# Decay rows spread over the partitions by DMA instead of by TensorE, with one exponential on 32 rows

## The reference

```python
# state space, per head, within a chunk of 128; a = dt * a_head
a_cum = jnp.cumsum(a, axis=-1)
seg = a_cum[..., :, None] - a_cum[..., None, :]
Lmat = jnp.exp(jnp.where(causal, seg, -jnp.inf))
CB = jnp.einsum('bclgn,bcsgn->bgcls', Cc, Bc)
y_diag = jnp.einsum('bgcls,bgecls,bcsgep->bclgep', CB, Lmat, X)
y_off = jnp.einsum('bclgn,bcgepn,bgecl->bclgep', Cc, prev, jnp.exp(a_cum))
# delta rule, per head, within a chunk of 64
G = jnp.cumsum(gc, axis=-1)
gamma = jnp.exp(jnp.where(tri, G[..., :, None] - G[..., None, :], -jnp.inf))
A = jnp.where(strict, jnp.einsum("bnhid,bnhjd->bnhij", kc * bc[..., None], kc) * gamma, 0.0)
```

## Time and profile before

| | |
|---|---|
| median of 3 runs | 2864.24 us (2861.77 to 2864.45) |
| the profiled execution, its own time | 2860.19 us |
| its span in the profile | 2858.4 us |
| TensorE busy | 2618.0 us, 92% |
| VectorE busy | 1500.9 us, 53% |
| ScalarE busy | 1125.3 us, 39% |
| GpSimd busy | 125.9 us, 4% |
| moved by DMA | 209.93 MB, 73 GB/s over the span |

### The profile page before, as it was taken

The page is one execution under the profiler, slowest core; times in us unless marked ns, Lnnn a source line. Parts: engine busy times, 40 slices in busy tenths (PEclk is TensorE's granted clock), DMA queues, the critical chain, the costliest instruction groups (busy, mean ns, idle before and its releaser), DMA issues. The chain is left out here.

```text
span 2858.4 us, 33690 instructions
## 1 busy us (share of the span) xinstructions
PE 2618.0 (92%) x13778; PEld 2044.9 (72%) x13778; DVE 1500.9 (53%) x2280; ACT 1125.3 (39%) x1687; POOL 125.9 (4%) x98
## 2 busy tenths in 40 slices
PE   8999978998998999988999978988898997899998
PEld 6888846766776776767888846756667675688886
DVE  5444266656566664345443254587644445466632
ACT  4222234555544455443222234242424255344422
POOL 0000020000000000010000020000000000100000
PEclk9999989999999999999999988999999998999999
DMA  4333312221221221222233311111111110233332
GB/s 139 97 102 91 101 52 69 67 68 58 82 72 47 74 67 59 82 81 74 96 96 98 94 54 59 53 52 38 52 38 45 60 59 23 74 96 96 98 99 76
DMA packets 59193, 209.93 MB, mean 73 GB/s; under 512 B 6560, under 2 KB 6560, under 8 KB 59040
## 3 DMA queue, kind: packets, MB, share of 16 engines
q1 hardware_dynamic: 57600, 204.38, 22.8%
q10 hardware_dynamic: 1440, 3.41, 0.3%
HBM read 205.66 MB, written 2.10 MB: 73 GB/s over the span
## 5 line engine op out<-in xcount | busy, mean ns | idle before, releaser
L1349 PE MATMUL bank<-uR,hl 128*128 128x512 f32 x2232 | 923.2, 414 | 54.5 <-DVE uR L1962 27.1
L1350 PE MATMUL bank<-uR,hl 128*128 128x512 f32 x2232 | 885.6, 397 | 0.0
L1351 PE MATMUL bank<-uR,hl 128*128 128x512 f32 x2232 | 884.5, 396 | 0.0
L1950 DVE TENSOR_TENSOR hl<-raw,hl 128x1024 fp32r<-128x1024 f32 (+1 forms) x391 | 473.1, 1210 | 618.1 <-ACT hl L1668 617.3
L1349 PEld LDWEIGHTS bank<-uR,hl 128*128 128x128 f32 x2232 | 429.0, 192 | 189.9 <-issue 67.5
L1668 ACT CAST hl<-raw 128x1024 fp32r<-128x1024 f32 (+1 forms) x391 | 402.4, 1029 | 249.4 <-PE bank L1351 248.3
L1351 PEld LDWEIGHTS bank<-uR,hl 128*128 128x128 f32 x2232 | 428.2, 192 | 93.7
L1350 PEld LDWEIGHTS bank<-uR,hl 128*128 128x128 f32 x2232 | 429.2, 192 | 85.9 <-issue 5.2
L1349 PE MATMUL bank<-act,hl 128*128 128x512 f32 x528 | 205.4, 389 | 0.0
L1350 PE MATMUL bank<-act,hl 128*128 128x512 f32 x528 | 205.4, 389 | 0.0
L1351 PE MATMUL bank<-act,hl 128*128 128x512 f32 x528 | 205.4, 389 | 0.0
(11 more groups left out here) (434 smaller groups left out, 2595.3 us busy)
## 6 DMA issues: line engine op xcount, KB each, us to landing
raw<-in_win SPq DMA_DIRECT2D x147, 512.0 KB, 3.5
raw<-in_w SPq DMA_DIRECT2D x44, 512.0 KB, 3.5
raw<-in_w1g SPq DMA_DIRECT2D x22, 512.0 KB, 3.5
raw<-in_w1u SPq DMA_DIRECT2D x22, 512.0 KB, 3.5
raw<-in_w2g SPq DMA_DIRECT2D x22, 512.0 KB, 3.5
raw<-in_w2u SPq DMA_DIRECT2D x22, 512.0 KB, 3.5
raw<-in_w1d SPq DMA_DIRECT2D x16, 512.0 KB, 3.5
raw<-in_wssd SPq DMA_DIRECT2D x16, 512.0 KB, 3.6
```

Source lines behind the costliest of these rows:

```text
L1349: e.matmul(s.bank[:, :], h[:, 0, w], hi, start=s.first and q == 0, stop=False)
L1350: e.matmul(s.bank[:, :], h[:, 0, w], lo, start=False, stop=False)
L1351: i = e.matmul(s.bank[:, :], h[:, 1, w], hi, start=False, stop=s.last and q == n - 1)
L1950: e.tensor_tensor(h[:, 1, 0:s.width], x[:, 0:s.width], h[:, 0, 0:s.width].bitcast(F), ALU.subtract).then_inc(*sig("dve_split.lo", s))
```

## The change

The rows are spread by DMA. A new step `spread`, issued by ScalarE, copies rows of a page in SBUF to a page over 128 or 2 x 64 partitions; it waits for the row, for the readers of the slot's last use (8 semaphore slots, taken in turn) and for the page's last readers. In the state space the copies of a round (two E of one row each, one EA of two rows) are issued together: round 0 ahead of `ssd_x`, round 1 ahead of the four rounds, rounds 2 and 3 after `ssd_y` of rounds 0 and 1. EA's exponential is no longer taken on 128 partitions each time: `decay` takes it once on the 32 rows into a page `eac`, whose rows are copied. In the delta rule both spreads of a pair are issued at the start of `gdn_prep`. VectorE's subtraction and minimum of a head become four instructions of 128 columns that do both. The pages `ac` and `eac` are held to the end of the fourth group, the pools have 27 in place of 24 extra pages, and `mR` pages 16 and 17, `idR`, `selR`, `ssd_sel` and the step that filled `idR` go.

```diff
-NB1, NB2, NA = 24, 24, 11
+NB1, NB2, NA = 27, 27, 11
+NROW = 8
...
+    def spread(to, src, ready, rows):
+        n = row_next["n"] % NROW
+        row_next["n"] += 1
+        use = row_uses[n]
+        step("spread", to=to, src=src, ready=ready, rows=rows, slot=n, free=list(use[1]))
+        use[0] += 16 * len(rows)
+        to.t = [(f"row{n}_in", None, use[0])]
+        return n
...
     def ssd_core(g):
...
+        def begin(e2):
+            for hh in (2 * e2, 2 * e2 + 1):
+                E = fp.take()
+                Es.append((E, spread(E, ac, ac.t, [(8 * g + hh, 0, 128)])))
+            EA = fp.take()
+            EAs.append((EA, spread(EA, eac, eac.t, [(8 * g + 2 * e2, 0, 64), (8 * g + 2 * e2 + 1, 64, 64)])))
+
+        begin(0)
...
+        begin(1)
         for e2 in range(4):
-            b, EA, b2 = SB.take(), fp.take(), SB.take()
+            b2, (EA, n) = SB.take(), EAs[e2]
...
-            yield
+            if e2 < 2:
+                begin(e2 + 2)
+            yield
...
     def gdn_prep(p, hs):
+        gm, AT = fp.take(), gp.take()
+        n = spread(gm, nar, nar.t, [(2 * p, 0, 64), (2 * p + 1, 64, 64)])
+        n2 = spread(AT, nar, nar.t, [(32 + 2 * p, 0, 64), (33 + 2 * p, 64, 64)])
         yield from both(l2(k[0], 1.0, k2, 0), l2(k[1], 1.0, k2, 1), l2(q[0], DSC), l2(q[1], DSC))
...
 TensorE
-        def ssd_front(s):
-            one = idR[0:32, s.H:s.H + 1].broadcast_to([32, 128])
-            e.matmul(s.b[:, :], one, mR[0][0:32, 16, :], start=True, stop=False)
-            e.matmul(s.b[:, :], one, mR[0][0:32, 17, :], start=False, stop=True).then_inc(*sig("pe_ssd.cum", s))
...
-            e.matmul(s.b[:, :], selR[:, s.i, :], mR[0][0:32, 16, :], start=True, stop=False)
-            e.matmul(s.b[:, :], selR[:, s.i, :], mR[0][0:32, 17, :], start=False, stop=True).then_inc(*sig("pe_ssd.ea", s))
...
-                t = e.matmul(s.b[r, :], con[1][0:32, h:h + 1].broadcast_to([32, 64]), s.nar[0:32, :], start=True, stop=True)
...
-                t = e.matmul(s.bb[r, :], con[1][32:64, h:h + 1].broadcast_to([32, 64]), s.nar[32:64, :], start=True, stop=True)
...
 ScalarE
-            e.copy(mR[0][0:32, 16, :], s.ac[0:32, :]).then_inc(*sig("act_ssd.achi", s))
+            after(*s.eac.after)
+            activate(s.eac[0:32, :], s.ac[0:32, :], ACT.Exp).then_inc(*sig("act_ssd.eac", s))
+
+        def spread(s):
+            after(*s.ready, *s.free, *s.to.after)
+            for row, first, n in s.rows:
+                e.dma_start(s.to[first:first + n, :], s.src[row:row + 1, :][:, None, :].broadcast_to([1, n, L])).then_inc(sem(f"row{s.slot}_in"), 16)
...
-            activate(s.EA[:, :], s.b[:, :], ACT.Exp).then_inc(*sig("act_ssd.EA", s))
...
 VectorE
-            e.tensor_tensor(v3(s.E), v3(s.b), over(n3(acN)[:, :, s.H][:, :, None], 128), ALU.subtract).then_inc(*sig("dve_ssd.seg", s))
-            e.tensor_scalar(s.E[:, :], s.E[:, :], 0.0, None, ALU.min).then_inc(*sig("dve_ssd.min", s))
+            after(*s.et)
+            for t in range(T4):
+                x = e.tensor_scalar(s.E[:, tcol(t)], s.E[:, tcol(t)], n3(acN)[:, t, s.H:s.H + 1], 0.0, ALU.subtract, ALU.min)
+            x.then_inc(*sig("dve_ssd.min", s))
...
-            e.tensor_tensor(v8(s.gm), v8(s.b), col(gcol, s.p), ALU.subtract).then_inc(*sig("dve_gdn.seg", s))
+            e.tensor_tensor(v8(s.gm), v8(s.gm), col(gcol, s.p), ALU.subtract).then_inc(*sig("dve_gdn.seg", s))
...
-            e.tensor_tensor(s.AT[:, :], s.gm[:, :], s.bb[:, :], ALU.mult).then_inc(*sig("dve_gdn.beta", s))
+            e.tensor_tensor(s.AT[:, :], s.AT[:, :], s.gm[:, :], ALU.mult).then_inc(*sig("dve_gdn.beta", s))
```

More of the change, by code:

```diff
@@ L324, in rstd @@
         return r
+    row_uses = [[0, []] for _ in range(NROW)]
+    row_next = {"n": 0}
+    def spread(to, src, ready, rows):
[6 more added lines that the diff above has]
+        return n
     def side_rstd(src, which):
@@ L569, in decay_side @@
         dt = S1["dt"]
-        e1, w, ln, a, ac = fp.take(), fp.take(), fp.take(), fp.take(), fp.take()
-        s = step("decay", dt=dt, e1=e1, w=w, ln=ln, a=a, ac=ac, after=t_phase)
+        e1, w, ln, a, ac, eac = fp.take(), fp.take(), fp.take(), fp.take(), fp.take(), fp.take()
+        s = step("decay", dt=dt, e1=e1, w=w, ln=ln, a=a, ac=ac, eac=eac)
+        ac.t, eac.t = [("dve_ssd.scan", s)], [("act_ssd.eac", s)]
         e1.release(("dve_soft.s5", s))
@@ L581, in decay_side @@
         dt.release(("pe_ssd.decay", s2))
-        ac.release(("pe_ssd.decay", s2), ("dve_ssd.aclo", s))
-        S1["decay"], S1["cum"] = s2, s
+        S1["decay"], S1["ac"], S1["eac"] = s2, ac, eac
     def project_group(g):
@@ L598, in project_group @@
         yield
-    S1["sel"] = []
     def ssd_core(g):
@@ L604, in ssd_core @@
         xs, B, C = G["xs"], G["B"], G["C"]
-        dec, cum = S1["decay"], S1["cum"]
-        s_sel = step("ssd_sel", g=g, after=list(S1["sel"]))
-        Xd = []
+        dec, ac, eac = S1["decay"], S1["ac"], S1["eac"]
+        Xd, Es, EAs = [], [], []
+        def begin(e2):
[5 more added lines that the diff above has]
+        begin(0)
         for t in range(T4):
@@ L630, in front @@
         def front(hh):
-            b, E = SB.take(), fp.take()
-            s = step("ssd_front", H=8 * g + hh, b=b, E=E, CB=CB, cum=cum, dec=dec)
+            E, n = Es[hh]
+            s = step("ssd_front", H=8 * g + hh, E=E, et=list(E.t), CB=CB, dec=dec)
             E.t = [("dve_ssd.E", s)]
-            b.release(("dve_ssd.seg", s))
-            return E
-        Es = [front(0)]
+            row_uses[n][1] = list(E.t)
+        front(0)
         yield
-        Es.append(front(1))
+        front(1)
         yield
@@ L666, in ssd_core @@
             EA.release(*Y[e2].t)
-            S1["sel"] = [("pe_ssd.ea", s_f)]
+            row_uses[n][1] = list(Y[e2].t)
             yield
             if e2 < 3:
-                Es += [front(2 * e2 + 2), front(2 * e2 + 3)]
+                front(2 * e2 + 2)
+                front(2 * e2 + 3)
                 yield
             yb = SB.take()
-            s_y = step("ssd_y", e2=e2, Xd=Xd, E=[Es.pop(0), Es.pop(0)], yb=yb, Y=Y[e2], yt=list(Y[e2].t))
+            s_y = step("ssd_y", e2=e2, Xd=Xd, E=[Es[2 * e2][0], Es[2 * e2 + 1][0]], yb=yb, Y=Y[e2], yt=list(Y[e2].t))
             for x in s_y.E:
@@ L988, in gdn_prep @@
             yield
-        gb, gm = SB.take(), fp.take()
-        s1 = step("gdn_decay", p=p, nar=nar, cols=cols, b=gb, gm=gm)
-        gb.release(("dve_gdn.seg", s1))
+        s1 = step("gdn_decay", p=p, cols=cols, gm=gm, gt=list(gm.t))
+        row_uses[n][1] = [("dve_gdn.seg", s1)]
         yield
-        bb, AT, kk, qk = SB.take(), gp.take(), SB.take(), SB.take()
-        s2 = step("gdn_att", p=p, nar=nar, k=k2, q=q, bb=bb, AT=AT, kk=kk, qk=qk, gm=gm, s=s1)
-        bb.release(("dve_gdn.beta", s2))
+        kk, qk = SB.take(), SB.take()
+        s2 = step("gdn_att", p=p, k=k2, q=q, AT=AT, at=list(AT.t), kk=kk, qk=qk, gm=gm, s=s1)
+        row_uses[n2][1] = [("dve_gdn.beta", s2)]
         AT.t = [("dve_gdn.AT", s2)]
@@ L1916, in scalar_program @@
               "conv": conv, "decay": decay, "decay_turn": decay_turn, "ssd_cb": ssd_cb, "ssd_state": ssd_state,
-              "ssd_front": ssd_front, "ssd_from": ssd_from, "silu_ev": silu_ev, "tanh_ev": tanh_ev, "half_ev": half_ev,
+              "ssd_front": ssd_front, "spread": spread, "silu_ev": silu_ev, "tanh_ev": tanh_ev, "half_ev": half_ev,
               "qkv_ev": qkv_ev, "gate_out": out_hi, "att_out": out_hi, "merge1": out_hi, "merge2": out_hi, "lam": lam_,
@@ L2146, in ssd_from @@
         def ssd_from(s):
-            go.wait_ge(*on("act_ssd.EA", s))
+            after(*s.et)
             go.wait_ge(*on("pe_ssd.off", s))
```

58 lines of the change are left out of this document (11 added, 47 removed).

## The result

| | before | after |
|---|---|---|
| median | 2864.34 us (2861.77 to 2864.68) | 3086.99 us (3085.10 to 3087.44) |
| ratio, 95% interval | | 1.0778 (1.0759 to 1.0797) |
| span of the profiled execution | 2858.4 us | 3085.2 us |
| TensorE busy | 2618.0 us | 2621.7 us |

The change costs 222.6 us. Lines moved: L1349, L1350, L1351 of before are now L1376, L1377, L1378; `ssd_x` is L1416, the matmuls of `ssd_from` L1441, `ssd_y` L1450; ScalarE's split is L1671 and VectorE's L1948; the copies are issued at L1769. VectorE's multiplication with `CB`, the last step to `E`, is L2138, and every activation of ScalarE is L1654. The median before is of four runs here, one more than ahead of the prediction.

The account below looks back on a forecast made before the run. TensorE's instruction order bounds the kernel; with copies, four state-space groups need 477.6 us instead of 347.2, +130.4, less the delta rule's 8.5: +122, 2986 us. The 8-in-10 range was 2820 to 3085.

Parts of the forecast that it names:

- what is removed: TensorE: matmuls taken out save 32.8 us in four state-space groups and 8.5 in the delta rule, 41.3 us of work.
- VectorE nothing: State-space heads: four 128-column instructions add 1 to 17 us over 32 heads, covered by VectorE's idle time, so nothing.
- the price of a copy: State-space copies: 256 KB read from one partition takes 9.7 us, at 27 GB/s.
- The bound of 2.1 us: Lower bound for a 256 KB copy, from output transfers with 128 partitions at both sides.
- twelve copies set a group's length: State space: a group can't be shorter than 12 x 9.7 = 116.4 us plus some 3; four groups +130.4 us.
- ScalarE's issues: ScalarE: 80 DMA issues at 0.52 us, 42 us, some 34 in the state-space stretch; nothing, with cover.
- The sentence on what stands behind an issue: An issue waiting for its page delays the L1668 split, L1950 and TensorE; taken as nothing, 48 us at 3 us each.
- the 119.4: Shortest state-space group in us: twelve copies, 116.4, plus some 3 for first issue and last exponential, multiply and matmul.
- the delta rule, -8.5: Delta rule: matmuls for the spreads of decays removed, 8.5 us saved, with its copies hidden.
- The read is not limited: State-space copies take 2.1 to 6 us, TensorE binds again: -35 to -41 us, about 2826; chance 0.29.
- The copies also starve the weights: State-space groups: a weight panel takes 9.7 us while copies flow, another +140 us, 3125; chance 0.13.
- ScalarE's waits at the issues: Fast copies, but 16 issues wait 3 us each: 48 us against the gain of 41, 2871; chance 0.04.

Follow-up runs that it names:

- e3: Changed kernel with the copied rows written once to HBM and every copy reading its row there, same queue and moments: 2834.92 us, ratio 0.9906 to the kernel before.
- e8: Kernel before with VectorE's part alone, subtraction and minimum as four 128-column instructions still reading PSUM: 2862.89 us, ratio 0.9999.
- e1: Changed kernel with state-space copies reading a constant page over as many partitions as they write, delta rule's copies unchanged: 2855.35 us, ratio 0.9978 to before.
- e5: Changed kernel with ac and eac copied again 64 partitions further on, half of every spread reading the twin: 2967.95 us, ratio 1.0368 to before.
- e6: Changed kernel with ac and eac copied again 32 partitions further on, half of every spread reading the twin: 3088.39 us, ratio 1.0786 to before.
- e2: Changed kernel with the copies issued by GpSimd in place of ScalarE, sources and order unchanged: 3009.56 us, ratio 1.0515 to before.
- e4: Kernel before with the delta rule's part of the change alone, row copies issued by ScalarE: 2884.90 us, ratio 1.0081.
- e11: e3 with the copies issued by GpSimd: 2830.36 us, ratio 0.9890 to the kernel before.
- e7: e3 with the delta rule as in the kernel before, its decays by matmuls: 2835.80 us, ratio 0.9905 to the kernel before.
- e12: e7 with the copies issued by GpSimd: 2831.04 us, ratio 0.9891 to the kernel before.

## Why the prediction came out as it did

**Right: what is removed.** The matmuls are gone, and where nothing stands in their place (e3) the groups lose 28.5 of the 32.8 us forecast, and TensorE's busy time 37.5 of the 41.3.

**Right: VectorE nothing.** 1.13 against 1.11 us a head, and e8 shows no change.

**Right: the price of a copy.** 9.7 us, at 26 to 28 GB/s. e1 moves the source alone and takes the cost away; e5 and e6 show that the place read sets it. The bound of 2.1 us was near for a source spread over the partitions (2.5 us).

**Not borne out: twelve copies set a group's length.** The forecast's group has rounds 29 us apart with TensorE at `ssd_y`. In after the rounds stand 10 to 34 us apart, with 81.4 us of such waits, but the copies' queue also runs empty. In e2 the lengths agree, 115.1 to 123.4 us for 119.4, and the mechanism doesn't: TensorE waits 6.7 us there, and late weight panels fill the rest. As far as the runs show, that agreement is luck; the copies may still set the length through the weight loads beside them, which no run separates.

**Wrong: ScalarE's issues.** This is the step that failed: "64 + 16 = 80 DMA issues in ... 0.52 each: 42 us ... Nothing, with cover". The 0.52 us came from eight loads spread over the partitions, whose queue never backed up; it is right for a copy that lands in 3.8 us (0.45 to 0.63 in e3). With a copy of 9.7 us the issuing engine itself stands, 265.5 / 16 = 16.6 us at a burst, 265.5 us where the forecast had some 34 for the stretch. "Issuing two steps ahead fills the queue, it doesn't shorten it" was true of the copies and wrong of what fills: after two DMAs the next is paid for by ScalarE's time. The sentence on what stands behind an issue (the split at L1668, VectorE's L1950, TensorE) named the right chain and priced only waits for pages. It is the chain of 88.7 us. And the held engine is late with the next burst, so the copies themselves don't run back to back, as the 119.4 assumed: 20 us of empty queue in the second group. Issuing from GpSimd ends it, and the groups become 95.7 us shorter. The span missed the forecast's by 226.8 - 121.9 = 104.9 us; 542.8 - 477.6 = 65.2 of that lies in the groups and 8.0 ahead of and between them.

**Wrong: the delta rule, -8.5.** It was +23 (e4), by the same hold. This is the remaining 31.6 us of the miss, 23.1 + 8.5.

**Not foreseen: the clock.** Idle stretches of 11 to 21 us are followed by matmuls at half the rate, 38 us more busy time than the same matmuls take in e3. This is inside the figures above, not beside them: it is why TensorE's busy time did not fall. No run separates it from the waits that go before it.

**The rivals.** "The read is not limited" is false, but the gain it named, 35 to 41 us, is near what e11 finds once the source is changed, 31. "The copies also starve the weights" is real as a mechanism (11.4 us to landing in after, 41.4 in e2), and costs 5 us of ScalarE's waits in after and 175 in e2, where it sets the length of the groups. Its total, 3125, lay nearer than the forecast's, for another reason. "ScalarE's waits at the issues" was a rival only together with fast copies, and as waits for pages; the real one needs slow copies and came on top of the likeliest case instead of beside it.

**A smaller slip.** ScalarE's queue carries 14.7 MB more (18.09 against 3.41), not 21: 32 rows of 256 KB and 48 halves of 128 KB are 14.7 MB. No term rested on it.

**Open.** Whether copies of 9.7 us alone, with neither a hold nor late weights, would make the groups 119.4 us long was not tried. Why the delta rule gains nothing from 8 us fewer matmuls (e3 against e7, e11 against e12) wasn't settled. How many bytes or descriptors the queue takes before it holds was seen only as "two DMAs pass", with 128 and with 256 KB; no other sizes were run. How the +222.6 us divides between late panels, late copies and the clock is known only as far as e2 and e3 divide it.

## What to carry to other kernels

Ask of a DMA not only how many bytes it moves but how many partitions it reads and writes: one row read 128 times goes at 27 GB/s, and the same row in HBM lands in 3.8 us. An issue is cheap only while the queue drains; count what stands behind it on the issuing engine at the copy's full price, and give such copies to an engine on which nothing waits. Where something keeps a queue from filling without bound, look at what it protects before taking it away: off ScalarE the copies delayed the weight loads instead.

## What the runs showed of the hardware

- Reading one partition for a copy to 128: 26 to 28 GB/s. A twin 64 partitions away: 53 to 61. A twin 32 away: no gain.
- One 2 KB row of HBM read 128 times: 256 KB in 3.8 us (ScalarE's queue) and 4.3 us (GpSimd's).
- ScalarE's queue takes two such slow DMAs in 0.5 and 0.6 us; the third then holds the engine for about 7 us and the fourth, in a row, for 9.7. With copies that land in 3.8 us no issue took longer than 0.63 us.
- GpSimd's queue took such copies without holding the engine, 0.5 to 0.6 us each: 512 KB loads on SyncE's queue then landed after 41.4 us (median of two), against 11.4 beside ScalarE's and 3.5 without slow copies.
- After 15.69 us idle TensorE's matmuls stepped 0.43 us apart instead of 0.23.
